# Filler matmuls between the first stage's last adaLN tiles, and five side jobs of each mixer moved by one unit

## What is computed

```python
for l in range(DEPTH):                                   # DEPTH = 2
    mod = (c @ w_ada[l] + b_ada[l])                      # adaLN: 9 blocks of 1024 per layer
    h = ada_norm(x, norm_gain[l, 0], shift0, scale0)     # rmsnorm(x, g) * (1 + scale) + shift
    x = x + 0.5 * gate0 * swiglu(h, w_ffn_in[l, 0], w_ffn_out[l, 0])
    h = ada_norm(x, norm_gain[l, 1], shift1, scale1)
    y, states = mixer_block(h, ...)   # branch A (HGRN2), branch B (RG-LRU), branch C (GLA), merge gates
    x = x + gate1 * y
    h = ada_norm(x, norm_gain[l, 2], shift2, scale2)
    x = x + 0.5 * gate2 * swiglu(h, w_ffn_in[l, 1], w_ffn_out[l, 1])
y = rmsnorm(x, final_norm)
```

## Time and profile before

| | |
|---|---|
| median of 3 runs | 1452.62 us (1451.72 to 1453.42) |
| the profiled execution's own time | 1452.93 us |
| its span | 1451.1 us |
| TensorE (PE) busy | 1431.5 us, 99% of the span |
| DVE, ACT, POOL busy | 923.0, 807.7 and 87.5 us |
| the chain that ended last | 92% on PE |
| mean DMA rate | 223 GB/s |

### The profile page before, as it was taken

How to read it: one execution, slowest core, us unless ns; L and a number is a source line. 1 busy time by engine, 2 the same in 40 slices (tenths; PEclk the granted TensorE clock), 3 DMA queues, 4 the chain that set the end, 5 groups by cost and what they waited for, 6 DMA issues and landing times.

```text
span 1451.1 us, 33412 instructions
## 1 busy us (share of the span) xinstructions
PE 1431.5 (99%) x14126; PEld 1369.3 (94%) x14126; DVE 923.0 (64%) x1572; ACT 807.7 (56%) x1337; POOL 87.5 (6%) x131
## 2 busy tenths in 40 slices
PE   6999999999999999999999999999999999999998
PEld 4999999998999999999999999999999999999998
DVE  3655446788875687555576545577798677755553
ACT  2553435887666466444464444468866755644543
POOL 1030000001110110000000000000111002000000
PEclk9999999999999999999999999999999999999999
DMA  9988897698994669788668888776999558775661
GB/s 340 287 253 271 248 272 196 169 259 245 244 243 145 183 186 289 216 248 252 193 189 267 278 278 256 193 192 189 263 249 270 166 153 222 218 233 166 173 190 41
DMA packets 460038, 323.77 MB, mean 223 GB/s; under 512 B 11219, under 2 KB 435707, under 8 KB 459890
## 3 DMA queue, kind: packets, MB, share of 16 engines
q1 hardware_dynamic: 452240, 299.96, 70.8%
q0 software_dynamic: 6880, 20.41, 5.2%
q10 hardware_dynamic: 770, 1.27, 0.2%
HBM read 313.29 MB, written 8.37 MB: 222 GB/s over the span
## 4 chain that ended last, share of the span: by engine, by line
PE 92%; DVE 3%; ACT 2%; SPq 1%; DMA 1%; issue 1%; DVEq 0%; ACTq 0%
PE bank L492 28%; PE bank L493 27%; PE bank L494 27%; PE bank L678 4%; SPq L550 1%; DVE wlo L457 1%; PE bank L841 1%; DMA first<-in_w_ada 1%; PE bank L869 1%; PE bank L888 1%; ACT whi L449 0%; PE bank L910 0%; PE bank L689 0%; DMA raw<-in_w_in 0%; PE bank L845 0%
## 5 line engine op out<-in xcount | busy, mean ns | idle before, releaser
L457 DVE TENSOR_TENSOR wlo<-raw,whi 128x1024 fp32r<-128x1024 f32 (+1 forms) x436 | 518.3, 1203 | 346.9 <-ACT whi L449 346.2
L492 PE MATMUL bank<-hH,whi 128*128 128x264 f32 x2048 | 587.9, 287 | 0.3 <-DVE wlo L457 0.3
L493 PE MATMUL bank<-hL,whi 128*128 128x264 f32 x2048 | 581.3, 284 | 0.1
L494 PE MATMUL bank<-hH,wlo 128*128 128x264 f32 x2048 | 580.9, 284 | 0.0
L449 ACT ACTIVATE whi<-raw 128x1024 fp32r<-128x1024 f32 (+1 forms) x436 | 442.2, 1033 | 187.2 <-PE bank L494 175.5
L492 PEld LDWEIGHTS bank<-hH,whi 128*128 128x128 f32 x2048 | 386.0, 188 | 13.7 <-issue 12.2
L493 PEld LDWEIGHTS bank<-hL,whi 128*128 128x128 f32 x2048 | 386.4, 189 | 0.0
L494 PEld LDWEIGHTS bank<-hH,wlo 128*128 128x128 f32 x2048 | 384.5, 188 | 0.2 <-issue 0.2
L492 PE MATMUL bank<-hidH,whi 128*128 128x264 f32 x704 | 201.4, 286 | 0.0
L494 PE MATMUL bank<-hidH,wlo 128*128 128x264 f32 x704 | 200.4, 285 | 0.0
L493 PE MATMUL bank<-hidL,whi 128*128 128x264 f32 x704 | 199.8, 284 | 0.0
(11 more groups left out here) (323 smaller groups left out, 1658.6 us busy)
## 6 DMA issues: line engine op xcount, KB each, us to landing
raw<-in_w_ffn_in SPq DMA_DIRECT2D x176, 512.0 KB, 4.9
raw<-in_w_in SPq DMA_DIRECT2D x120, 512.0 KB, 5.5
ring<-in_w_ada SPq DMA_DIRECT2D x96, 512.0 KB, 6.6
raw<-in_w_ffn_out SPq DMA_DIRECT2D x64, 512.0 KB, 4.9
raw<-in_w_ada SPq DMA_DIRECT2D x32, 512.0 KB, 4.3
raw<-in_w_ffn_out SPq DMA_DIRECT2D x32, 384.0 KB, 4.8
first<-in_w_ada SPq DMA_DIRECT2D x16, 512.0 KB, 12.4
raw<-in_w_out SPq DMA_DIRECT2D x16, 512.0 KB, 5.2
```

The costliest lines, as they stand in the source:

```text
L457: nc.vector.tensor_tensor(wlo[:, s, 0:w], raw[:, r, 0:w], whi[:, s, 0:w].bitcast(F), ALU.subtract).then_inc(lo_done, 1)
L492: nc.tensor.matmul(out, a, rh, start=start, stop=False)
L493: nc.tensor.matmul(out, a, rl, start=False, stop=False)
L494: return nc.tensor.matmul(out, b, rh, start=False, stop=stop)
```

## The change

It has these parts.

1. At the start the last group of `first` is split, so that tiles 13 and 14 have one semaphore and tile 15 its own. Five filler matmuls run between tiles 12 and 13, two between tiles 14 and 15; the four behind tile 15 stay. The wait for `set_dve` moves ahead of the first fillers, since they write the bank that DVE copied.
2. ACT splits unit 1 after it has written `hH`, no longer before.
3. TensorE runs the 16 matmuls of unit 1 that need only `whi` first and waits for its `wlo` behind them.
4. In both mixers the adaLN group at u = 10 goes to 11 and that at 29 to 28, C's value transposes go from u = 32 and 34 to 31 and 33, and the fourth samples' output from 44 to 43. DVE's and ACT's work on these moves along by one unit.

```diff
-FIRST_GROUPS = (range(0, 8), range(8, 11), range(11, 13), range(13, 16))
+FIRST_GROUPS = (range(0, 8), range(8, 11), range(11, 13), range(13, 15), range(15, 16))
...
-MIX_ADA = (10, 16, 29, 71)
+MIX_ADA = (11, 16, 28, 71)
...
-AT = {... 'C_vT': (32, 34), ... 'so': (24, 28, 38, 44, 47, 52), ...}
+AT = {... 'C_vT': (31, 33), ... 'so': (24, 28, 38, 43, 47, 52), ...}
...
-                    unit_ready(pe, n)
+                    hi_first = (L, f, k) == (0, 0, 1)
+                    if hi_first:
+                        pe.wait_ge(hi_done, n + 1)
+                    else:
+                        unit_ready(pe, n)
...
-                    for kt in range(KT):
+                    for kt in range(KT) if hi_first else ():
+                        a = whi[:, n % SLOTS, kt * P:(kt + 1) * P]
+                        mm(BK[b][:, 0:NT], a, hH[:, kt], start=(kt == 0), stop=False)
+                        mm(BK[b][:, 0:NT], a, hL[:, kt], start=False, stop=False)
+                    for kt in range(KT) if hi_first else ():
+                        if kt == 0:
+                            unit_ready(pe, n)
+                        last = mm(BK[b][:, 0:NT], wlo[:, n % SLOTS, kt * P:(kt + 1) * P], hH[:, kt],
+                                  start=False, stop=(kt == KT - 1))
+                    for kt in range(0 if hi_first else KT):
...
-            ada_units(8, 8)
+            ada_units(8, 5)
             pe.wait_ge(set_dve, 2)
+            keep_warm(5)
+            ada_units(13, 2)
+            keep_warm(2)
+            ada_units(15, 1)
             keep_warm(WARM)
...
             split_hi(act, 0)
-            split_hi(act, 1)
             wait(act, "mod_ready", 0, 1)
...
+            split_hi(act, 1)
             split_hi(act, 2)
```

More of the change, by code:

```diff
@@ L119 @@
 LOAD_AT = {load: c for c, load in enumerate(LOADS)}
-AT = {'ca': 9, 'alpha': 11, 'A_vT': 14, 'A_sT': 16, 'C_sT': 30, 'C_vT': (32, 34), 'A_out': 50, 'C_out': 56, 'A_kT': 59, 'A_S': 63, 'C_kT': 68, 'C_S': 70, 'tailT': 73, 'kv': (22, 26, 35, 40, 45, 50), 'st_f': ((13, 14), (15, 16), (31, 32), (36, 37), (43, 44), (48, 48)), 'k_v': ((21, 21), (26, 26), (34, 35), (39, 40), (44, 45), (49, 50)), 'so': (24, 28, 38, 44, 47, 52), 'st': (14, 17, 33, 37, 44, 48)}
+AT = {'ca': 9, 'alpha': 11, 'A_vT': 14, 'A_sT': 16, 'C_sT': 30, 'C_vT': (31, 33), 'A_out': 50, 'C_out': 56, 'A_kT': 59, 'A_S': 63, 'C_kT': 68, 'C_S': 70, 'tailT': 73, 'kv': (22, 26, 35, 40, 45, 50), 'st_f': ((13, 14), (15, 16), (31, 32), (36, 37), (43, 44), (48, 48)), 'k_v': ((21, 21), (26, 26), (34, 35), (39, 40), (44, 45), (49, 50)), 'so': (24, 28, 38, 43, 47, 52), 'st': (14, 17, 33, 37, 44, 48)}
 EARLY_AT = {'A_abs': 7, 'A_ln': 9, 'A_ls': 9, 'A_exp': 10, 'A_k': 11, 'A_f': 10, 'C_z': 10, 'C_ln': 15, 'C_ls': 16, 'C_f': 19, 'conv': (9, 10, 14, 15), 'conv_hi': 18, 'conv_lo': 19, 'A_qs': 15, 'C_qs': 17}
```

## The result

The changed kernel takes **1461.84 us** (median of 4 runs, 1461.36 to 1463.01) against 1452.61 before (4 runs): ratio 1.0063, 95% interval 1.0051 to 1.0075, or **9.2 us slower**. The prediction was 1454.1 with a range up to 1456.7, so it was wrong. The profiled execution has a span of 1459.6 us (1451.1 before).

The account below looks back on a forecast made before the run. TensorE, busy for 99% of the span, was taken to bound the kernel. Start -0.85 us and +1.2 us in each mixer, twice +2.4, gave +1.5 us in all: 1454.1 us, range 1450.4 to 1456.7.

Parts of the forecast that it names:

- the last sentence of part 4: Mixers, u = 10 to 11: unit 14's load comes earlier, unit 16's later; counted as nothing.
- B: Mixers, unit 32's load takes 5.1 us, DVE 3.2 us late: 1456.6 us in all; chance 17 in 100.
- The term at u = 33: Mixers: unit 32's late load delays DVE by 2.0 us and the level; +1.6 us in each mixer.
- The joins: Mixers: side jobs placed behind other work at 11 and 43 save 0.2 us each, in each mixer.
- The start: First stage: clock stays at 1.00, unit 0 starts 0.5 us earlier and unit 1 0.85 us earlier; -0.85 us.
- The seven fillers eat nearly all that the clock gives back: Start, around tiles 13 to 15: fillers hold the clock but leave only 0.1 us of gain.
- a join saves nothing there: Mixers, value transposes: they cost 0.36 us of TensorE, no more than their work, so joining them gains nothing.
- rival A: Mixers: unit 32's load in time or its delay hidden, transposes fill the 0.43 us wait; 1449.7 us, 14 in 100.

Follow-up runs that it names:

- Run 1: Kernel before with only the adaLN group at u = 10 moved to 11, its loads moving along: 1459.61 us against 1452.74.
- run 2: Kernel before with the adaLN group at 11 on TensorE, its four loads kept in their old order: 1452.65 us against 1452.74.
- run 3: Kernel before with only the adaLN group at 29 moved to 28 in both mixers: 1458.62 us, +5.9 us.
- run 9: Kernel before with only the start's parts 1 to 3 of the change, mixers as before: 1452.65 us against 1452.74.
- run 10: Kernel before with the changed start but without the seven new fillers, mixers as before: 1451.01 us against 1452.80.
- run 7: Kernel before with only C's value transposes at 31 and 33 and the samples' output at 43: 1451.48 us against 1452.80.
- run 6: Kernel before with the adaLN group at 28 and C's value transposes at 31 and 33: 1459.46 us against 1452.35.
- run 8: Two kernels, each the whole change with one undoing: loads of the group at 11 in old order, 1456.48 us; group of 28 back at 29, 1456.46 us.
- run 4: Kernel before with the adaLN group kept at 29 on TensorE, only its four loads moved ahead of unit 32's load: 1459.36 us against 1452.35.
- run 5: Kernel before with the adaLN group at 28 on TensorE, its four loads in their old place: 1460.54 us against 1452.80.

## Why the prediction was wrong

- **The step that failed** is the last sentence of part 4: "The same shift at u = 10 to 11 goes the other way for unit 14, whose load comes earlier, and delays that of unit 16, whose split DVE has ready more than one unit ahead; I count nothing." The direction was right, and unit 16 itself did not start late. What was not looked at is what stands behind unit 16's load in the same queue: three loads and the four tiles of the next group, which go straight to TensorE, without three units of lead. Before, the last of them landed 1.4 us ahead of its use. In the trace the term is 2.1 us in the first mixer and 2.8 in the second, for nothing predicted. Run 1 with the new order of the loads and run 2 with the old one differ in nothing else, and by 1459.61 - 1452.65 = 7.0 us. No rival had this mechanism; B was at u = 33.
- **The term at u = 33** was right in mechanism and place, and near in size: ACT's wait 3.94 (3.5 predicted), DVE's 2.14 (2.0), TensorE's 2.46 in the second mixer (2.2), 1.11 in the first behind the pause of 0.86. The load took 4.1 and 4.0 us where I took 3.9. The steps at u = 31 to 34 sum to 2.9 us in the trace, for 3.2 predicted. By the medians it costs 4.7 us (9.2 - 4.5); with some 2.5 us of uncertainty that is not told from 3.2. ("It idles 2.2 us instead of 0.6" misreads the row, which has 0.43; the sum does not use it.)
- **The clock behind such a wait** is nowhere in the sum. In run 3 each wait was followed by 1.3 to 1.5 us of it. In the profiled execution of the changed kernel it did not fall (mean granted clock 0.998). The other three executions show 0.993 to 0.995 and took 0.3 to 1.7 us longer, which fits one fall or more in each; no trace of them shows where.
- **The fit of the Trainium skill** ("DMA: Bandwidth & Descriptors", anatomy of one DMA), 2.0 us and the bytes over 436 GB/s for GpSimd's path, would have given 3.2 us for this load, as an estimate. The measured 4.0 and 4.1 decide against it on SP's queue.
- **The joins**: 0.13 at 11 and 0.09 at 43 for 0.2 each; small and right in sign in the steps, too small for the medians.
- **The start**: the clock stayed at 1.00 as said. Against the start of tiles 8 to 12 in each trace (25.86 before, 26.21 after), `adaT` gained nothing for 0.1 predicted, unit 0 gained 0.2 for 0.5, unit 1 0.6 for 0.85. The median of run 9 has 0.1 where I had 0.85, and its interval, -1.5 to +1.0 us, holds both. "The seven fillers eat nearly all that the clock gives back" was right for the changed kernel and too kind to them: run 10 shows that they eat more, 1.2 us in the trace and 1.7 by the medians.
- **The value transposes**: "a join saves nothing there" was right for the join; that they fill the wait of 0.43 was in rival A only, and it shows in the trace of run 7.
- **The 1.2 us behind u = 47** in the first mixer appear in none of the part runs by more than 0.15 us. The level waits for DVE's `xC`. The chain of work followed back from that level goes over DVE's and ACT's splits to a load for the samples, `xA<-v_rows`, which landed late. ACT waited for two such loads; in the kernel before and in the 14 other runs it waits for neither at this place by more than 0.3 us:

```profile
400.03 1.28 ACT L1240 ACTIVATE st<-st,bC 128x128 f32<-128x128 f32 x4 [1.12 <-DMA st<-in_state_gla]
...
405.48 1.28 ACT L1240 ACTIVATE xA<-xA,kC 128x128 f32<-128x128 f32 x4 [1.16 <-DMA xA<-v_rows]
```

  The second took 10.6 us from issue to landing, and 8.8 before. What made it slower stays open.
- **Left open.** Pauses of TensorE without a releaser ("issue") of 0.3 to 1.3 us sit at other units in nearly every kernel (u = 24, 26 or 28). Those of the changed kernel sum to 1.9 us and that of the kernel before to 0.6. They have one thing in common: of the 20 such pauses of over 0.25 us between 50 and 1430 us in all 16 traces, 18 end 1.2 to 1.5 us after a packet of the instruction queue (q8, 16 KB) has arrived, though one comes only every 13 us on the mean. Ahead of the pause that ends at 346.76 it arrives at 345.55, and at 1046.29 ahead of the one that ends at 1047.59. So they read like waits for instructions; nothing was tried that moves them alone.

## What to carry over

When a load moves in a list that reuses slots, work out for every load within one turn of the slots which release it now waits for, and then follow each late one through the whole queue: the victim is the next consumer without lead, which may be a job that nobody moved. Price a new wait of TensorE of about 2 us or more with the clock behind it: here the clock fell behind ten of the eleven new waits of 2.15 us or more in the mixers. A filler is free only until the thing it waits for has landed; look at when the real work could have started, not at the clock.

## What the hardware showed that was not expected

- In the mixers the granted clock fell to 0.50 (1.2 GHz) behind single waits of TensorE of 2.15 and 2.41 us (run 6), 2.18 (run 1), 2.40 (run 8, second mixer), 2.56 twice (run 4), 2.79 and 2.83 (run 3), 2.98 and 3.41 (run 5), and behind four tiles with waits of 0.31, 0.65 and 0.67 between them (run 8, with the group back at 29). In the changed kernel it did not fall behind 2.46, nor behind 0.17, 0.66 and 0.65 between the same four tiles, and in the first mixer of run 1 not behind 0.45, 0.75 and 0.86 there. The length of the wait alone does not decide. By the step at the unit behind, a fall cost 1.0 to 1.5 us, and in run 6 1.6 and 2.1 (the step there would be -0.36 without it, for the transposes that moved away).
- Medians of parts need not add up: 6.9 + 5.9 - 0.1 - 1.3 = 11.4, for a whole of 9.2. With an uncertainty of some 3 us on the sum the two do not contradict each other. That the falls of the clock differ from kernel to kernel is in the traces, and from execution to execution only in the mean clock of the changed kernel's four (0.998, 0.993, 0.995, 0.995).
- SP's queue landed seven loads of 512 KB in 11.8 us in the first mixer, at the same mean of 311 GB/s whether they began 3 us earlier or later, and in the second mixer in 12.4 us instead of 10.4. A delay at the head of such a run arrived at its end undiminished or grown.
